# Two small SBUF tables get longer rows, so that every large tile behind them starts on a multiple of 128 bytes

## The chip, the cores and the metric

One Trainium2 chip, one of its cores. The metric is the time of one execution on the device in microseconds (us). Inputs are laid out in memory on the host before the launch; that is not timed.

## The reference

Three blocks in a row work on 256 tokens of 1024 features, all in float32. The first block has two layers. Layer 0 is differential attention over 256 context tokens and the 256 tokens themselves, layer 1 is a pooling over windows of tokens; each is followed by a SwiGLU network, and both are modulated by vectors made from a condition `c`. The second block mixes a gated linear attention and a block-sparse attention, and is followed by a wide network (1024 to 4096 and back) and a gated embedding.

```python
x = layer_norm(ALPHA * x + g1 * y_lat, ...)                # attention or pooling
x = layer_norm(ALPHA * x + g2 * swiglu(modulate(x, sh2, sc2), ffn_w_in[i], ffn_w_out[i]), ...)
...
x = x + (sigmoid(gate_a) * y_a + sigmoid(gate_b) * y_b) @ w_out
x = x + square(relu(rms_norm(x) @ w_up)) @ w_down
x = x + sigmoid(rms_norm(x) @ w_ple_gate) * (p @ w_ple)
```

## The kernel before

Nearly all the time goes into products of a 256-row activation with a large weight matrix. To get float32 accuracy from TensorE's faster float32 type (`f32r`, printed as f32 in the rows), every factor is split into a high and a low part, and a product is three matmuls: high by high, high by low, low by high.

- **Weights** stream from memory into a ring `raw` (six slots of 2048 floats per partition; the queue of SyncE, SP, issues these transfers in the order of use). ScalarE rounds a piece to its high part `wH` (line 638), VectorE subtracts and writes the low part `wL` (line 1213). A piece ("sub") is 128 x 1024.
- **Activations** are transposed by TensorE and split in the same way into a pair of tiles. `aHL` holds high and low part of the 1024-feature activations of most stages; `cH`, `cL` those of the context; `hH`, `hL` the hidden activations of SwiGLU (22 blocks of 128 features); `uH`, `uL` those of the wide network (32 blocks); `oa` and `pH`, `pL` two smaller ones.
- **Two ways to multiply.** In `three` (lines 2068 to 2070) the activation is the stationary operand (128 columns of it are loaded as weights, LDWEIGHTS, engine PEld in the rows) and 512 columns of the weight matrix stream past as the moving operand. In `columns_T` (lines 2103 to 2105, 256 columns) and `chunk_mm_halves` (lines 2136 and 2138) it is the other way round: a piece of `wH` or `wL` is stationary and the activations move.

```python
def three(outp, xh, xl, h, l, first, last_, part_of=False):
    T.matmul(outp, xh, h, ...)             # line 2068
    T.matmul(outp, xh, l, ...)             # line 2069
    return T.matmul(outp, xl, h, ...)      # line 2070
```

The first operand after the output is the stationary one. A row of the trace names them in another order: `ps<-wH,hH` at line 2068 is a matmul with `hH` stationary and `wH` moving; at line 2103, `ps<-cH,wH` has `wH` stationary and `cH` moving.

The stages in order: q, k, v of the attention (v with `cH` and `aHL` by turns, 192 matmuls), attention heads, its output product, `in0` and `out0` (SwiGLU of layer 0), pooling, `in1` and `out1`, the input product `win` of the second block with the linear attention in between, `bra` with the sparse attention in between (its stationary tile is `oa`), `brb`, `wo2`, `up`, `down` (stationary `uH`, `uL`), `pg`, `ple` (stationary `pH`, `pL`). `out0` and `out1` have `hH`, `hL` stationary. `rows_mm` runs those with an activation stationary: per block of 128 features and per half of the tokens two times three matmuls.

Between two matmuls that belong to a stage TensorE waits only for `w_lo` (VectorE has split the sub), for the transposed activations (`t_lo`, `h_lo`) and for a free bank of PSUM (`acc_out`). `idle_mm` (line 2222) issues matmuls of `hH` by `hH` whose result is not used, where TensorE would stand still at the end of a layer norm.

**Where tiles stand.** The tiles are allocated in the order of the code, each at the next multiple of 32 bytes behind the one before; some share their place with tiles of other stages. The built program has them at these bytes of a partition, modulo 128:

| tiles | before | after |
|---|---|---|
| `raw`, `wL`, `wH`, `aHL`, `x`, `cst` (in front of the two tables) | 0 | 0 |
| `modraw`, `lnp`, `tf`, `modrow`, `modcol` (behind `cols`) | 96 | 0 |
| `cb`, `cT`, `wPool1`, `v`, `qT`, `kT`, `cH`, `cL`, `ot`, `ex`, `mod0`, `sh1b`, `sc1b`, `wPool0`, `hH`, `hL`, `sh` (behind `cols` and `vcol`) | 32 | 0 |
| second block: `xn`, `oa`, `laH`, `laL`, `tabr`, `u`, `uH`, `uL`, `hu`, `pH`, `pL`, `gate` (behind `cols`) | 96 | 0 |

Of the kernel before, what the change touches and what calls it, by code (L numbers as in the profile page):

```python
# [34 lines left out]
P = 128  # L35
D = 1024
KT = D // P
# [56 lines left out]
VECS = [(0, 2), (0, 3), (0, 4), (0, 5), (1, 0), (1, 1), (1, 2), (1, 3), (1, 4), (1, 5)]  # L94
# [107 lines left out]
def build(nc, a, cst_d, pool_d, out):  # L202
    ctx = ExitStack()
    with ctx:
        def sem(name):
            return ctx.enter_context(nc.semaphore(name))

        def sb(stack, name, shape, dt=fp32):
            return stack.enter_context(nc.sbuf_tensor(name, shape, dt))
# [12 lines left out]
        eps = sb(ctx, "eps", [P, 2])  # L222
        bn = sb(ctx, "bn", [P, TT, 12])
        mv = sb(ctx, "mv", [P, TT, 2])
        cols = sb(ctx, "cols", [P, 113])

        gcol = sb(ctx, "gcol", [P, 82])

# [6 lines left out]
        sA = ExitStack()  # L235
# [11 lines left out]
        esum = modrow[:, 0:32].rearrange("p (m r) -> p m r", m=2)  # L247
        einv = modrow[:, 32:48]
        modcol = sb(sA, "modcol", [P, 2, 4, KT, 2])
        vcol = sb(sA, "vcol", [P, len(VECS) * KT])  # L250
        cb = sb(sA, "cb", [P, D])
        bcol = cols[:, 16:112]
        cT = sb(sA, "cT", [P, KT, 32])
# [118 lines left out]
        ctx_in, cols_in, cst_in, cst2_in = (sem(n) for n in ("ctx_in", "cols_in", "cst_in", "cst2_in"))  # L372
# [248 lines left out]
        def _(act):  # L621
# [68 lines left out]
                nc.scalar.activation(modrow[:, :], ps[:, 6, :], ACT.Copy).then_inc(mod_row, 1)  # L690


            act.dma_start(cols[:, :], a["cols"]).then_inc(cols_in, 16)
            act.dma_start(cst[:, 0:C_DIST], cst_d[:, 0:C_DIST]).then_inc(cst_in, 16)
            act.wait_ge(cols_in, 16)
            act.wait_ge(cT_zero, 1)
# [2063 lines left out]
```

## Time and profile before

| | before |
|---|---|
| median of three runs | 1114.23 us (1114.17 to 1116.12) |
| the profiled execution, its own time | 1114.73 us |
| its span, from the first to the last instruction | 1113.0 us |
| TensorE busy (share of the span) | 1099.3 us (99%) |
| VectorE, ScalarE busy | 776.3 us (70%), 587.0 us (53%) |
| granted TensorE clock | 0.999, that is its 2.4 GHz level all through |
| moved by DMA | 238.31 MB, 214 GB/s in the mean |

A busy row of PE reaches from a matmul's start to its modelled end, and matmuls overlap: what counts for the time is the distance from one start to the next, called pitch below. A matmul of 512 columns streams for 512 / 2.4 GHz = 213.3 ns, one of 256 for 106.7 ns.

### The profile page before, as it was taken

What the parts mean: (1) busy time and instruction counts of PE and PEld (TensorE: products, weight loads), DVE (VectorE), ACT (ScalarE), POOL (GpSimd) and SP (SyncE); (2) the same over time, 40 slices, a digit from 0 to 9 for tenths busy, and PEclk for the clock granted to TensorE, in tenths of its full rate; (3) what the DMA queues carried; (4) which work ended last, traced back from release to release, by engine and by line L of the source; (5) the groups of instructions that cost most, each with busy time, mean ns of one, the idle gap of its engine ahead of it and who ended that gap; (6) DMA issues with size and microseconds to landing.
All of it is one profiled execution on the core that took longest, in us unless ns stands there. A gap on an engine that the chain in (4) does not pass through costs nothing.

```text
span 1113.0 us, 14486 instructions
## 1 busy us (share of the span) xinstructions
PE 1099.3 (99%) x5851; PEld 910.0 (82%) x5851; DVE 776.3 (70%) x1007; ACT 587.0 (53%) x821; POOL 61.4 (6%) x118
## 2 busy tenths in 40 slices
PE   8999999999999999999999999999999999999998
PEld 4688766899998887888887878878888888888886
DVE  2596588889889797877745865455566677774454
ACT  3742376563454347555534767556754466563342
POOL 0011200002121001000000000000000000000000
PEclk9999999999999999999999999999999999999999
DMA  9987740679999946667567788786524455555541
GB/s 363 403 309 249 243 163 1 208 255 349 379 383 332 350 146 232 224 211 269 183 199 126 223 177 190 155 180 134 177 76 152 152 196 203 207 189 189 189 161 38
DMA packets 111986, 238.31 MB, mean 214 GB/s; under 512 B 5712, under 2 KB 51920, under 8 KB 110640
## 3 DMA queue, kind: packets, MB, share of 16 engines
q1 hardware_dynamic: 97280, 185.42, 53.2%
q0 software_dynamic: 14352, 51.72, 13.1%
q8 instruction: 46, 0.75, 0.3%
q10 hardware_dynamic: 288, 0.26, 0.1%
q14 instruction: 20, 0.16, 0.0%
HBM read 236.29 MB, written 1.07 MB: 213 GB/s over the span
## 4 chain that ended last, share of the span: by engine, by line
PE 92%; DVE 3%; DMA 3%; ACT 1%; issue 0%; SPq 0%; ACTq 0%
PE ps L2068 19%; PE ps L2069 19%; PE ps L2070 19%; PE ps L2136 10%; PE ps L2138 5%; PE ps L2105 4%; PE ps L2104 4%; PE ps L2103 4%; PE ps L2253 2%; DMA raw<-in_attn_w_qkv 2%; PE ps L2388 1%; PE ps L2356 1%; DMA raw<-in_qkv_first 1%; DVE wL L1213 1%; PE ps L2277 0%; PE ps L2621 0%
## 5 line engine op out<-in xcount | busy, mean ns | idle before, releaser
L1213 DVE TENSOR_TENSOR wL<-raw,wH 128x1024 fp32r<-128x1024 f32 x326 | 394.7, 1222 | 211.3 <-ACT wH L638 208.9
L638 ACT ACTIVATE wH<-raw 128x1024 fp32r<-128x1024 f32 x326 | 340.3, 1058 | 300.4 <-PE ps L2070 196.1
L2068 PE MATMUL ps<-wH,aHL 128*128 128x512 f32 x576 | 229.3, 398 | 2.4 <-DVE aHL L1616 0.9
L2069 PE MATMUL ps<-wL,aHL 128*128 128x512 f32 (+1 forms) x592 | 229.0, 387 | 0.0
L2070 PE MATMUL ps<-wH,aHL 128*128 128x512 f32 x576 | 224.8, 390 | 0.0
L2136 PE MATMUL ps<-aHL,wH 128*128 128x512 f32 x480 | 168.8, 397 | 0.0
L2068 PEld LDWEIGHTS ps<-wH,aHL 128*128 128x128 f32 x576 | 108.1, 188 | 35.1 <-issue 7.1
L2138 PE MATMUL ps<-aHL,wL 128*128 128x256 f32 x480 | 134.1, 279 | 0.0
L2069 PEld LDWEIGHTS ps<-wL,aHL 128*128 128x128 f32 x592 | 111.3, 188 | 20.8
L2070 PEld LDWEIGHTS ps<-wH,aHL 128*128 128x128 f32 x576 | 108.1, 188 | 23.4
L2136 PEld LDWEIGHTS ps<-aHL,wH 128*128 128x128 f32 x480 | 90.1, 188 | 21.7
L1289 DVE SCALAR_TENSOR_TENSOR modraw<-modraw,cb 128x1024 f32<-128x1024 f32 x80 | 96.4, 1219 | 4.4 <-DMA modraw<-in_mod_rows 4.3
L2138 PEld LDWEIGHTS ps<-aHL,wL 128*128 128x128 f32 x480 | 90.5, 188 | 0.0
L2103 PE MATMUL ps<-aHL,wH 128*128 128x256 f32 x288 | 81.7, 284 | 0.0
L2105 PE MATMUL ps<-aHL,wL 128*128 128x256 f32 x288 | 81.5, 283 | 0.0
L2104 PE MATMUL ps<-aHL,wH 128*128 128x256 f32 x288 | 81.5, 283 | 0.0
L2068 PE MATMUL ps<-wH,hH 128*128 128x512 f32 x176 | 70.0, 397 | 0.0
L2069 PE MATMUL ps<-wL,hH 128*128 128x512 f32 x176 | 69.6, 395 | 0.0
L2070 PE MATMUL ps<-wH,hL 128*128 128x512 f32 x176 | 69.2, 393 | 0.0
L555 POOL DMA_DIRECT2D modraw<-in_mod_rows x80 | 42.4, 531 | 367.8 <-DVE modraw L1289 313.4
L2103 PEld LDWEIGHTS ps<-aHL,wH 128*128 128x128 f32 x288 | 55.3, 192 | 0.0
L2104 PEld LDWEIGHTS ps<-aHL,wH 128*128 128x128 f32 x288 | 55.3, 192 | 0.0
(330 smaller groups left out, 1491.7 us busy)
## 6 DMA issues: line engine op xcount, KB each, us to landing
raw<-in_ffn_w_in SPq DMA_DIRECT2D x88, 512.0 KB
modraw<-in_mod_rows POOLq DMA_DIRECT2D x80, 512.0 KB, 6.6
raw<-in_w_in SPq DMA_DIRECT2D x32, 1024.0 KB
raw<-in_ffn_w_out SPq DMA_DIRECT2D x22, 1024.0 KB
raw<-in_w_up SPq DMA_DIRECT2D x16, 1024.0 KB
raw<-in_w_down SPq DMA_DIRECT2D x16, 1024.0 KB
mod<-in_mod_first SPq DMA_DIRECT2D x8, 1024.0 KB, 16.8
raw<-in_attn_w_qkv SPq DMA_DIRECT2D x8, 1024.0 KB
```

The source lines that it names most:

```text
L555: pool.dma_start(modraw[:, n % MT, :], a["mod_rows"][v, k, :, :]).then_inc(mod_in[n % MT], 16)
L638: nc.scalar.activation(wHigh(n), raw[:, (n // 2) % RAW, (n % 2) * 1024:(n % 2) * 1024 + 1024], ACT.Copy).then_inc(w_hi, 1)
L1213: V.tensor_tensor(wL[:, n % WL, :], raw[:, (n // 2) % RAW, (n % 2) * 1024:(n % 2) * 1024 + 1024], wHigh(n).bitcast(fp32), ALU.subtract).th ...
L1289: V.scalar_tensor_tensor(out=tile, in0=tile, scalar=1.0, in1=cb[:, :], op0=ALU.mult, op1=ALU.mult, accum_out=vcol[:, n:n + 1]).then_inc(ve ...
L2068: T.matmul(outp, xh, h, start=first, stop=False, skip_group_check=part_of)
L2069: T.matmul(outp, xh, l, start=False, stop=False, skip_group_check=part_of)
L2070: return T.matmul(outp, xl, h, start=False, stop=last_, skip_group_check=part_of)
L2103: T.matmul(dst, h, x_h[:, k, :], start=k == 0 and b % 2 == 0, stop=False, skip_group_check=True)
L2104: T.matmul(dst, h, x_l[:, k, :], start=False, stop=False, skip_group_check=True)
L2105: ins = T.matmul(dst, l, x_h[:, k, :], start=False, stop=k == KT - 1, skip_group_check=True)
L2136: T.matmul(dst, wH[:, slot(n + s), c0:c0 + P], aHL[:, k, :, :].rearrange("p a s -> p (a s)"), start=k == 0, stop=False, skip_group_check=True)
L2138: ins = T.matmul(dst[:, S:2 * S], wL[:, (n + s) % WL, c0:c0 + P], aH[:, k, :], start=False, stop=k == KT - 1, skip_group_check=True)
```

## The change

`cols` (a table of 113 floats per partition: condition and biases) gets rows of 128 floats, of which the transfer fills the first 113 as before; `vcol` (80 floats per partition) gets rows of 96. No instruction is added, removed or moved on any engine. What changes in the program is the row length of these two tables and the start of everything that is allocated behind them: by 32 bytes behind `cols`, by 96 bytes behind `cols` and `vcol`.

```diff
-        cols = sb(ctx, "cols", [P, 113])
+        cols = sb(ctx, "cols", [P, P])
...
-        vcol = sb(sA, "vcol", [P, len(VECS) * KT])
+        vcol = sb(sA, "vcol", [P, 96])
...
-            act.dma_start(cols[:, :], a["cols"]).then_inc(cols_in, 16)
+            act.dma_start(cols[:, 0:113], a["cols"]).then_inc(cols_in, 16)
```

## Rows read from the trace of the kernel before

**Rows 1.** Page: busy time by engine; chain that ended last, by engine
```profile
PE 1099.3 (99%) x5851; PEld 910.0 (82%) x5851; DVE 776.3 (70%) x1007; ACT 587.0 (53%) x821; POOL 61.4 (6%) x118
PE 92%; DVE 3%; DMA 3%; ACT 1%; issue 0%; SPq 0%; ACTq 0%
```

**Rows 2.** One tile's matmuls: count, duration in ns (min/median/max), first and last start
```profile
L2068 PE MATMUL ps<-wH,hH x176: 392/395/494, 340.6 to 609.3; 128*128 128x512 f32 x176
L2068 PE MATMUL ps<-wH,uH x128: 392/395/476, 989.7 to 1079.5; 128*128 128x512 f32 x128
L2068 PE MATMUL ps<-wH,cH x32: 394/394/500, 97.8 to 141.8; 128*128 128x512 f32 x32
```

**Rows 3.** Timeline of PE, 512 columns: start us, duration us, instruction
```profile
199.34 0.39 PE L2069 MATMUL ps<-wL,aHL 128*128 128x512 f32 x1
...
207.95 0.39 PE L2068 MATMUL ps<-wH,aHL 128*128 128x512 f32 x1
...
355.13 0.39 PE L2069 MATMUL ps<-wL,hH 128*128 128x512 f32 x1
...
366.33 0.39 PE L2069 MATMUL ps<-wL,hH 128*128 128x512 f32 x1
...
1020.03 0.40 PE L2069 MATMUL ps<-wL,uH 128*128 128x512 f32 x1
...
1031.46 0.39 PE L2070 MATMUL ps<-wH,uL 128*128 128x512 f32 x1
```

**Rows 4.** Timeline of PE in v, where cH and aHL alternate
```profile
103.34 0.39 PE L2068 MATMUL ps<-wH,cH 128*128 128x512 f32 x1
...
106.14 0.40 PE L2068 MATMUL ps<-wH,aHL 128*128 128x512 f32 x1
...
108.67 0.40 PE L2070 MATMUL ps<-wH,aHL 128*128 128x512 f32 x1
```

**Rows 5.** Timeline of PE, 256 columns, in k, in0 and the pooling
```profile
50.01 0.28 PE L2103 MATMUL ps<-cH,wH 128*128 128x256 f32 x1
...
52.39 0.28 PE L2105 MATMUL ps<-cH,wL 128*128 128x256 f32 x1
...
300.07 0.28 PE L2104 MATMUL ps<-aHL,wH 128*128 128x256 f32 x1
...
308.95 0.28 PE L2103 MATMUL ps<-aHL,wH 128*128 128x256 f32 x1
...
410.48 0.28 PE L2068 MATMUL ps<-wPool,aHL 128*128 128x256 f32 x1
...
412.83 0.28 PE L2070 MATMUL ps<-wPool,aHL 128*128 128x256 f32 x1
```

**Rows 6.** Timeline of PE, first matmuls of 512 columns after transposes or small ones
```profile
196.96 0.48 PE L2068 MATMUL ps<-wH,aHL 128*128 128x512 f32 x1
...
199.11 0.39 PE L2068 MATMUL ps<-wH,aHL 128*128 128x512 f32 x1
...
404.26 2.54 PE L2222 MATMUL ps<-hH 128*128 128x512 f32 x10
```

**Rows 7.** Windows: stretch and its length, busy us of the engines, clock, DMA share, GB/s
```profile
989.70:1079.90 90.20, 90.20 (x393) 72.61 (x392) 43.57 (x41) 38.18 (x45) 0.00 (x0) 1.00 0.54 189
```

**Rows 8.** Timeline of DVE with its wait in brackets; longest waits (us in total, times, longest)
```profile
402.69 0.69 DVE L1548 TENSOR_TENSOR sh<-ps,g2b 128x512 f32<-128x512 f32 x1 [1.24 <-PE ps L2070]
...
DVE sh L1493 <- PE ps L2070: 9.0, 1, 9.0
```

**Rows 9.** Page, costliest groups: VectorE on tiles at 0 and at 96
```profile
L1213 DVE TENSOR_TENSOR wL<-raw,wH 128x1024 fp32r<-128x1024 f32 x326 | 394.7, 1222 | 211.3 <-ACT wH L638 208.9
L1289 DVE SCALAR_TENSOR_TENSOR modraw<-modraw,cb 128x1024 f32<-128x1024 f32 x80 | 96.4, 1219 | 4.4 <-DMA modraw<-in_mod_rows 4.3
```

**Rows 10.** Windows early in the kernel (columns as in rows 7, DVE, ACT, POOL included)
```profile
20.00:25.00 5.00, 5.00 (x32) 3.12 (x24) 1.78 (x4) 3.07 (x6) 0.00 (x0) 1.00 1.03 423
60.00:65.00 5.00, 5.00 (x39) 4.72 (x38) 5.00 (x6) 2.01 (x2) 0.00 (x0) 1.00 1.04 398
```

## The prediction

> **What bounds the kernel now.** I read the page first: TensorE is busy 99% of the span and makes up 92% of the chain that ended last; VectorE has 3% of it, DMA 3% [rows 1]. A change that touches no instruction can therefore bring something only if it changes how fast one matmul follows another, or one of the few places where the chain leaves TensorE. Busy time does not tell that, since matmuls overlap. So I went to the timeline of PE, picked stretches without any other instruction between the matmuls, and divided the time between two starts by the number of steps. In the built program nothing differs but start addresses, so I sorted the stretches by where their operands start.
>
> For 512 moving columns the reader is to see two levels [rows 3]. Between 199.34 and 207.95 us lie 38 steps with `aHL` stationary and `wH`, `wL` moving, all at 0 modulo 128: 8.61 / 38 = 226.6 ns a step. Between 355.13 and 366.33 lie 48 steps with `hH`, `hL` stationary (32 modulo 128): 11.20 / 48 = 233.3 ns. Between 1020.03 and 1031.46 lie 49 steps with `uH`, `uL` stationary (96 modulo 128): 11.43 / 49 = 233.3 ns. The moving operand is the same ring in all three, and the function is the same. In v the two kinds stand side by side [rows 4]: from the first matmul with `cH` at 103.34 to the first with `aHL` at 106.14 it is 12 steps in 2.80 us, 233.3 ns; the next 11, with `aHL`, take 2.53 us, 230.0 ns, so they start slow and end fast. The difference is thus 6.7 ns a matmul, 2.9%, and it comes with a stationary tile that does not start on a multiple of 128 bytes. It hardly comes with the load on other engines: in `down` VectorE is busy only 43.57 of 90.20 us and DMA 54% [rows 7], less than over the whole kernel for VectorE [rows 1], and the step is still the slow one.
>
> What exactly the address does can't be read. Two readings fit: (a) a weight load of 512 bytes per partition that starts off a 128-byte line costs 6.7 ns more; (b) it costs that when stationary and moving operand stand differently modulo 128. A third, (c), is that the address modulo 128 has nothing to do with it, and the tiles that lie further back in SBUF are slower, since all the slow ones lie behind byte 116,000 and `aHL` and the weights in front. There is one weak witness. `idle_mm` has both operands in `hH`, far back and both at 32. Ten of them after small matmuls take 2.54 us, less the 0.39 us of the last one's own duration 2.15 us for nine steps; nine steps with everything at 0 after transposes take 199.11 - 196.96 = 2.15 us too [rows 6]. Nine steps at the slow level would be 9 x 6.7 = 0.06 us more than at the fast one (less while such a run settles), so this speaks for (b) and against (c), by a difference of a few hundredths. (a) and (b) give the same after the change, since everything then stands at 0.
>
> **The change part by part.** Sum against the profiled execution, 1114.73 us, 0.5 us over the median of the three runs. The stationary tiles that move from 32 or 96 to 0:
>
> - `out1`: half of the `hH` matmuls. Rows 2 has 176 at line 2068; lines 2069 and 2070 have as many, 528 in all, 264 in each layer. 264 x 6.7 ns = 1.77 us. VectorE's first step behind it waits 9.0 us for TensorE [rows 8], so all of it counts.
> - `out0`: the same 1.77 us, but at its end VectorE's step on the last accumulators waits only 1.24 us for TensorE [rows 8]; if TensorE comes 1.77 us earlier, VectorE is late next, with the half before. I take 1.24 us.
> - `down`: 3 x 128 = 384 matmuls [rows 2], 2.57 us. TensorE is busy 90.20 of 90.20 us there [rows 7], and it is on the chain.
> - v: 3 x 32 = 96 matmuls with `cH` [rows 2], 0.64 us; and the 96 with `aHL` that alternate with them go from 230.0 to 226.6 ns [rows 4], 0.33 us.
> - `bra`, with `oa` stationary: 8 blocks x 2 halves x 2 x 3 = 96 matmuls by the code. The attention steps in between break them into runs of about twelve, and after a break even aligned ones step 2.15 / 9 = 239 ns at first [rows 6]. I take half, 0.3 us.
> - `ple`: 24 matmuls by the code, 0.16 us.
>
> Against it: where an activation moves, unlike starts seem no harm. 256 columns with `cH` moving (32) over `wH` (0) step 2.38 / 20 = 119.0 ns, with `aHL` (0) over `wH` (0) 8.88 / 74 = 120.0 ns; in the pooling, with `wPool` at 32 moving in two of three, 2.35 / 20 = 117.5 ns [rows 5]. If all become 120.0: 192 x 1.0 + 48 x 2.5 ns = 0.3 us lost. `in0`, `in1`, `up`, `win`, `brb`, `wo2` and `pg` have both operands in front of the tables and stay as they are.
>
> VectorE, ScalarE: an operation on tiles at 96 takes 1219 ns, one on tiles at 0 takes 1222 [rows 9], and these engines are 4% of the chain; nothing, covered by TensorE, and if it were not, 3 ns of 1222. DMA: while the transfers into `mod0` (32) and `lnp` (96) run among those into `raw`, 423 GB/s are moved, and 398 with `raw` alone as the target [rows 10]; the starts do not hurt, so nothing is to be had. The two tables themselves are read at the same width as before.
>
> Sum: 1.77 + 1.24 + 2.57 + 0.64 + 0.33 + 0.3 + 0.16 - 0.3 = 6.7 us. 1114.73 - 6.7 = 1108.0 for an execution like the profiled one, and **1107.5 us** from the median. Bounds of this case: all of `out0` and `bra` (0.9 us more) and no loss for moving operands (0.3 more) gives 1106.3; if `bra`, `ple` and the `aHL` part of v give nothing and `out0` half, 5.3 us, it is 1108.9.
>
> **The rivals.**
> - *The saving is partly taken back* by a wait. For: in `out0` the margin is the 1.24 us named, and weights arrive just in time in places. Against: in `down`, 2.57 us are in the clear. If `out0` and v gave nothing, 2.2 us of the 6.7 would be lost; with one more such place, `out1`, 4.0: from 1109.7 to 1111.5, say 1109 to 1112.
> - *No change.* Reading (c), or another property of the slow tiles. For: no row shows a tile that lies far back and starts at 0 modulo 128. Against: rows 6, weakly, and that tiles at 125,000 (`uH`) and at 204,000 bytes (`cH`) step alike. Time: 1114.2, or 1114.5 with the small loss above. The Trainium skill (SBUF — State Buffer, Door 1: The DMA port swizzle) has a rule that would also end here: SBUF is read in lines of 16 bytes, and what costs is to cross into a new line. By that rule a weight row of 512 bytes touches 32 lines from 0, 32 or 96 alike, no alignment beyond 16 bytes is worth anything, and the time stays 1114.2; the two levels in rows 3 are nothing that it explains.
> - *Slower.* Equal starts are what costs, and the 6.7 ns are of the place. For: the three 256-column rows, where the unlike ones are up to 2.5 ns faster than the like ones [rows 5]. For 512 columns that is up to 5 ns, on the 1128 matmuls with a moved stationary tile 5.6 us, and 0.3 us as above: 1120.1. It decides from 2.2 / 1128 = 2.0 ns a matmul. Against: rows 3 have the like pair faster by 6.7 ns at the very shape in question.
>
> **How the numbers follow.** A measurement of this kernel tells about 0.2% (2.2 us) from no change. The forecast 0.67 (its own range 1106 to 1109); partly taken back 0.14; no change 0.13; slower 0.04; and 0.02 for more gain than I see. Faster than 1112.0: 0.67 + 0.14 + 0.02 = 0.83; the same 0.13; slower 0.04. The range for 8 in 10 takes the forecast with its bounds and most of the second case: 1105.5 to 1111.5.
>
> **What the profile after would show.** 233.3 ns becomes 226.7 in `out0`, `out1` and `down`, the median duration of line 2068 with `hH` falls from 395 towards that of `aHL`, the matmuls with `aHL` stay as they are, and with `cH` moving the step becomes 120.0. `down` would last 90.2 - 2.6 = 87.6 us. The prediction is wrong if `uH` and `hH` keep their 233.3 ns (then it is the place), or if they reach 226.7 and TensorE shows new waits after `out0` or before the attention.

## The result and the profile after

| | before | after |
|---|---|---|
| median, same chip | 1114.9 us (1114.17 to 1116.12, 4 runs) | 1107.8 us (1106.66 to 1109.29, 4 runs) |
| the profiled execution, its own time and span | 1114.73, 1113.0 us | 1107.73, 1106.0 us |

The ratio is 0.9936, with an interval of 0.9919 to 0.9953: 7.1 us or 0.6% faster. A second measurement beside the experiments below gave 1106.63 us against 1114.97, 0.993 (0.9916 to 0.9943).

The page of after, busy time by engine and the chain that ended last, by engine, beside [rows 1]:

```profile
PE 1092.8 (99%) x5851; PEld 910.7 (82%) x5851; DVE 776.0 (70%) x1007; ACT 586.7 (53%) x821; POOL 61.6 (6%) x118
PE 87%; DVE 6%; DMA 4%; ACT 1%; SPq 1%; issue 1%; ACTq 0%; DVEq 0%
```

TensorE lost 6.5 us of its busy time; VectorE, ScalarE and the counts stand as before. The same matmuls of after as in [rows 2], count and duration in ns:

```profile
L2068 PE MATMUL ps<-wH,hH x176: 389/389/501, 339.4 to 605.1; 128*128 128x512 f32 x176
L2068 PE MATMUL ps<-wH,uH x128: 389/389/476, 985.3 to 1072.6; 128*128 128x512 f32 x128
L2068 PE MATMUL ps<-wH,cH x32: 389/389/499, 97.5 to 140.6; 128*128 128x512 f32 x32
```

The median fell from 394 or 395 to 389 ns. The steps say it better. PE's timeline of after: 48 steps in `out0`, 48 in `down`, 12 with `cH` and 12 with `aHL` in v, then 20 steps of 256 columns with `cH` moving and 20 in the pooling (for [rows 3 to 5]):

```profile
349.67 0.39 PE L2069 MATMUL ps<-wL,hH 128*128 128x512 f32 x1
...
360.55 0.39 PE L2069 MATMUL ps<-wL,hH 128*128 128x512 f32 x1
...
1009.82 0.39 PE L2068 MATMUL ps<-wH,uH 128*128 128x512 f32 x1
...
1020.70 0.39 PE L2068 MATMUL ps<-wH,uH 128*128 128x512 f32 x1
...
102.93 0.39 PE L2068 MATMUL ps<-wH,cH 128*128 128x512 f32 x1
...
105.65 0.39 PE L2068 MATMUL ps<-wH,aHL 128*128 128x512 f32 x1
...
108.37 0.39 PE L2068 MATMUL ps<-wH,cH 128*128 128x512 f32 x1
...
50.00 0.28 PE L2104 MATMUL ps<-cL,wH 128*128 128x256 f32 x1
...
52.40 0.28 PE L2103 MATMUL ps<-cH,wH 128*128 128x256 f32 x1
...
407.51 0.28 PE L2069 MATMUL ps<-wL,aHL 128*128 128x256 f32 x1
...
409.90 0.28 PE L2068 MATMUL ps<-wPool,aHL 128*128 128x256 f32 x1
```

The reader is to see 10.88 / 48 = 226.7 ns in `out0` and in `down` (before 233.3), 2.72 / 12 = 226.7 in v both with `cH` and with `aHL`, 2.40 / 20 = 120.0 with `cH` moving and 2.39 / 20 = 119.5 in the pooling. The window over `down` of after, beside [rows 7]:

```profile
985.30:1073.00 87.70, 87.70 (x393) 72.74 (x392) 43.58 (x41) 38.01 (x45) 0.00 (x0) 1.00 0.55 194
```

The same 393 matmuls with the engine never idle, 2.5 us sooner. From the first start of a stage's matmuls to the last, by the two traces, v went from 44.52 to 43.61 us (0.91), `out0` from 61.64 to 60.11 (1.53), `out1` from 62.25 to 60.53 (1.72), `bra` from 35.02 to 34.77 (0.25), `down` from 90.23 to 87.73 (2.50), `ple` from 5.37 to 5.21 (0.16). That is 7.07 us. The first weight product began 0.40 us earlier, at 16.05 us (the traces of this study have it between 16.05 and 16.70). By the starts of corresponding matmuls 0.4 us went back in the layer norm behind `out1`. There TensorE loads blocks of `x` to transpose them; before, that load came without a wait, after, it waits for VectorE (line 1512). The rows of PEld, before and after:

```profile
618.52 1.02 PEld L2253 LDWEIGHTS ps<-cst,x 128*128 128x128 f32 x8
```

```profile
614.72 0.86 PEld L2253 LDWEIGHTS ps<-cst,x 128*128 128x128 f32 x8 [0.40 <-DVE x L1512]
```

Another 0.2 us went back at the start of `in1` and 0.2 us came in at the start of `up`, where the matmuls of lines 2136 and 2138 changed their pace (more on them at the end). What is left over is 0.1 us. The span is 7.0 us shorter.

VectorE at the end of `out0`, beside [rows 8], wait in brackets:

```profile
396.82 0.68 DVE L1548 TENSOR_TENSOR sh<-ps,g2b 128x512 f32<-128x512 f32 x1
...
398.26 0.69 DVE L1556 BATCH_NORM_STATS2 bn<-x 128x6 f32<-128x512 f32 x1
...
399.96 0.69 DVE L1548 TENSOR_TENSOR sh<-ps,g2b 128x512 f32<-128x512 f32 x1 [1.00 <-PE ps L2070]
```

The last accumulators are taken 2.73 us earlier than before (402.69 then), and VectorE still waited 1.00 us for them. The 1.24 us of before were no limit: the work of VectorE ahead of that wait had come forward as well (the same step of line 1548 one half earlier started at 399.32 before and starts at 396.82 here). At its start, on the other hand, `out0` lost a little, since TensorE now waits there for VectorE to multiply the last hidden block (line 1737). PE of after:

```profile
341.14 0.50 PE L2068 MATMUL ps<-wH,hH 128*128 128x512 f32 x1 [0.17 <-DVE sh L1737]
```

### The profile page after: what moved, and what is told of

Read it like the earlier page. It is cut to its first block, busy times and chain, and to the rows that moved or that the text cites. A ratio compares the mean times of both kernels' runs of the same rounds, so it can differ in the third digit from the quotient of the medians.

```text
span 1106.0 us, 14486 instructions
## 1 busy us (share of the span) xinstructions
PE 1092.8 (99%) x5851; PEld 910.7 (82%) x5851; DVE 776.0 (70%) x1007; ACT 586.7 (53%) x821; POOL 61.6 (6%) x118
## 4 chain that ended last, share of the span: by engine, by line
PE 87%; DVE 6%; DMA 4%; ACT 1%; SPq 1%; issue 1%; ACTq 0%; DVEq 0%
PE ps L2068 19%; PE ps L2070 18%; PE ps L2069 18%; PE ps L2136 10%; PE ps L2138 5%; PE ps L2105 2%; PE ps L2104 2%; PE ps L2103 2%; DVE wL L1213 2%; PE ps L2253 2%; DMA raw<-in_qkv_first 2%; PE ps L2388 1%; PE ps L2356 1%; DMA raw<-in_ffn_w_in 1%; DMA raw<-in_w_in 1%; DVE modraw L1289 1%
## 5 line engine op out<-in xcount | busy, mean ns | idle before, releaser
L1213 DVE TENSOR_TENSOR wL<-raw,wH 128x1024 fp32r<-128x1024 f32 x326 | 395.1, 1222 | 207.1 <-ACT wH L638 204.5
L1289 DVE SCALAR_TENSOR_TENSOR modraw<-modraw,cb 128x1024 f32<-128x1024 f32 x80 | 96.5, 1219 | 3.9 <-DMA modraw<-in_mod_rows 3.8
```

The source lines that it names most:

```text
L1213: V.tensor_tensor(wL[:, n % WL, :], raw[:, (n // 2) % RAW, (n % 2) * 1024:(n % 2) * 1024 + 1024], wHigh(n).bitcast(fp32), ALU.subtract).th ...
L1289: V.scalar_tensor_tensor(out=tile, in0=tile, scalar=1.0, in1=cb[:, :], op0=ALU.mult, op1=ALU.mult, accum_out=vcol[:, n:n + 1]).then_inc(ve ...
```

## The experiments

d is from here on the start of an activation tile less the start of the ring (`wH` and `wL` are alike), modulo 256 bytes. In the kernel before d is 0 for `aHL`, -96 for `hH` and `cH`, -32 for `uH`, `oa`, `pH`; in after it is 0 for all. The kernels add unused tiles, or use a tile from a few floats further back; none leaves work out. Each added line shifts the line numbers by one. First four kernels on the question of the two readings (a) and (b).

**Everything moved by 32 bytes**, after with one pad in front of all:

```diff
+        sb(ctx, "pad0", [P, 8])
         sLow = ExitStack()
```

> The changed kernel with a pad of 32 bytes in front of everything: all large tiles, the weight ring and aHL included, stand at 32 modulo 128, so every stationary tile is off the 128-byte line but equal to its moving operand. Theory (a), a weight load that starts off a 128-byte line costs 6.7 ns: the 1728 matmuls of 512 columns with aHL stationary and the 1128 with the other activations step 233.3 instead of 226.7 ns, 19 us more, and those with the ring stationary lose as well: 1127 us or more. Theory (b), what costs is a stationary and a moving operand at unequal places modulo 128: all steps stay 226.7 and 120.0 ns, 1107.8 us. Theory (c), the place in SBUF: already contradicted by the change itself, would give 1107.8 too.

Measured: 1108.58 us (1106.52 to 1109.68), ratio to before 0.994 (0.9925 to 0.9954). All settled 512-column steps were 226.7 ns though no large tile stood on a multiple of 128 bytes. Reading (a) fell.

**The first edit alone**, made in the kernel before; `vcol` keeps its 80 floats:

```diff
-        cols = sb(ctx, "cols", [P, 113])
+        cols = sb(ctx, "cols", [P, P])
...
+            act.dma_start(cols[:, 0:113], a["cols"]).then_inc(cols_in, 16)
```

> Only cols is padded: the tiles of the second block (oa, uH, uL, pH, pL) stand at 0, those behind vcol (cH, cL, hH, hL, wPool0) at 64 modulo 128. If the unit is 128 bytes, down, bra and ple are fast (2.57 + 0.3 + 0.16 = 3.0 us less than before) and out0, out1 and v keep a step of about 233.3 ns: about 1111.8 us. If 64 bytes are enough, hH and cH step 226.7 too: 1107.8 us.

Measured: 1109.66 us (1108.11 to 1112.9), ratio 0.9956 (0.9941 to 0.9972). `uH` (d = 0) stepped 226.7 ns, `hH` and `cH` (d = -64) 228.9. With `cH` moving six of eight stretches stepped 117.8 and two 113.4, 116.7 in the mean. So there are more than two levels.

**The ring alone at 32**, after with 8 floats in front of `raw` and 24 behind `wH`:

```diff
+        sb(ctx, "pad0", [P, 8])
         sLow = ExitStack()
...
+        sb(ctx, "pad1", [P, 24])
```

> The changed kernel with the ring raw, wL, wH at 32 and everything else, aHL, hH and uH included, at 0 modulo 128. In lines 2068 to 2070 the stationary operand is then on the line and the moving one is not. Theory (a): they all step 226.7 ns; the ring is stationary in 1056 matmuls of 256 columns and 960 of lines 2136 and 2138, where up to 6.7 ns each are lost, 13.5 us: 1107.8 to 1121 us. Theory (b): 1728 + 1128 matmuls step 233.3 ns, 19 us more, and the 256-column ones of lines 2103 to 2105 step about 119 instead of 120.0 ns, 1 us less: 1126 us.

Measured: 1124.85 us (1124.43 to 1125.56), ratio 1.0088 (1.0073 to 1.0103). The activations stood on multiples of 128 bytes as in after; the two pads had pushed them by 128 bytes, so d is 96 for all of them. The timeline of PE in this kernel, 38 steps with `aHL` and 48 with `uH` stationary:

```profile
198.15 0.40 PE L2071 MATMUL ps<-wL,aHL 128*128 128x512 f32 x1
...
207.06 0.39 PE L2070 MATMUL ps<-wH,aHL 128*128 128x512 f32 x1
...
1017.43 0.39 PE L2070 MATMUL ps<-wH,uH 128*128 128x512 f32 x1
...
1028.68 0.39 PE L2070 MATMUL ps<-wH,uH 128*128 128x512 f32 x1
```

8.91 / 38 = 234.5 and 11.25 / 48 = 234.4 ns, where only the moving operand had moved. Reading (b) holds in kind.

**`aHL` alone at 32**, after with 8 floats in front of `aHL` and 24 behind it:

```diff
+        sb(ctx, "pad0", [P, 8])
         aHL = sb(ctx, "aHL", [P, KT, 2, S], f32r)
+        sb(ctx, "pad1", [P, 24])
```

> The changed kernel with aHL alone at 32, everything else at 0 modulo 128. Both theories (a) and (b): the 1728 matmuls with aHL stationary, 226.7 ns in both kernels so far, step 233.3 ns, 11.5 us more: 1119 us, which gives the cost a second time and in front part of SBUF. Where aHL moves (lines 2103 to 2105) (b) expects 119 instead of 120.0 ns, 1 us less, (a) no difference. Theory (c), the place: 1107.8.

Measured: 1117.94 us (1117.44 to 1119.8), ratio 1.0028 (1.0016 to 1.004). The timeline of PE, 38 steps with `aHL`, 48 with `hH` stationary:

```profile
198.24 0.40 PE L2072 MATMUL ps<-wH,aHL 128*128 128x512 f32 x1
...
207.11 0.40 PE L2071 MATMUL ps<-wL,aHL 128*128 128x512 f32 x1
...
352.61 0.40 PE L2072 MATMUL ps<-wH,hL 128*128 128x512 f32 x1
...
363.76 0.40 PE L2072 MATMUL ps<-wH,hL 128*128 128x512 f32 x1
```

`aHL` at 233.4 ns was expected; `hH` at 11.15 / 48 = 232.3 was not. The pads had pushed it and `uH` by 128 bytes, so they stood where (b) asks, alike modulo 128, and were slow. The unit is wider than I had written. The next kernels look for the period, with pads that put each group of tiles at a d of its own.

**d = 64, 256, 128** for `aHL`, first block, second block in after:

```diff
+        sb(ctx, "pad0", [P, 16])
         aHL = sb(ctx, "aHL", [P, KT, 2, S], f32r)
+        sb(ctx, "pad1", [P, 48])
...
+        sb(sB, "pad2", [P, 96])
```

> The changed kernel with pads only, so that the large tiles stand at chosen distances from the ring wH, wL (d = start of the tile less start of the ring, modulo 512): aHL at d = 64, cH, hH and wPool0 at d = 256, oa, uH, pH and laH at d = 128. Theory: the step of 512 columns follows d modulo 256. Then hH and cH stationary step 226.7 ns as at d = 0, uH again 232.4 as the tiles at d = 128 did in the run with aHL at 32, and aHL something near the 228.9 that d = -64 gave. Time about 1107.8 + 1728 x 2.2 ns + 504 x 5.7 ns - 864 x 3.3 ns (256 columns moving, if d = 64 gives 116.7 as d = -64 did) = 1111.6 us. Rival one: d counts modulo 512 or as the distance itself; then hH and cH are unlike too and step 232 to 234 ns, 3.6 us more, about 1115. Rival two: only multiples of 128 count and the 232.4 had another cause (the place): hH and uH both 226.7, about 1108.7.

**d = 256, 96, 64** for the same three groups:

```diff
+        sb(ctx, "pad0", [P, 64])
         aHL = sb(ctx, "aHL", [P, KT, 2, S], f32r)
+        sb(ctx, "pad1", [P, 64])
...
+        sb(sA, "pad2", [P, 24])
...
+        sb(sB, "pad3", [P, 16])
```

> The changed kernel with pads only: aHL at d = 256 from the ring, cH, hH, wPool0 at d = 96, oa, uH, pH at d = 64. Theory (d modulo 256): aHL stationary 226.7 and moving 120.0 as before; hH, cH 234.3 as the run with the ring at 32 gave for d = 96, 624 x 7.6 ns = 4.7 us; uH, oa, pH the same as aHL gives at d = 64 in the kernel beside it, near 228.9, 504 x 2.2 ns = 1.1 us: about 1113.6 us. Rival (modulo 512 or the distance itself): aHL is unlike at 232 to 234 ns, 1728 x 5.7 ns = 9.9 us more, about 1123.

Measured: 1118.44 us (1117.84 to 1120.17), ratio 1.0031 (1.0019 to 1.0043), and 1114.83 us (1114.29 to 1115.45), 0.9997 (0.9988 to 1.0006). The timeline of PE in the first of them, `hH` at d = 256, and of the second, `aHL` at d = 256 and `uH` at 64:

```profile
352.54 0.39 PE L2073 MATMUL ps<-wH,hL 128*128 128x512 f32 x1
...
363.42 0.39 PE L2073 MATMUL ps<-wH,hL 128*128 128x512 f32 x1
```

```profile
199.65 0.39 PE L2073 MATMUL ps<-wL,aHL 128*128 128x512 f32 x1
...
208.27 0.39 PE L2072 MATMUL ps<-wH,aHL 128*128 128x512 f32 x1
...
1012.60 0.40 PE L2073 MATMUL ps<-wL,uH 128*128 128x512 f32 x1
...
1023.80 0.40 PE L2073 MATMUL ps<-wL,uH 128*128 128x512 f32 x1
```

10.88 / 48 = 226.7 and 8.62 / 38 = 226.8 ns: 256 bytes apart is as good as 0, for tiles in front and at the back, while 128 apart is not. So the period is taken to be 256, and "modulo 512" fell; of the other values of d none was tried again 256 bytes further. My guess that +64 would equal -64 fell too: 11.20 / 48 = 233.3 instead of 228.9. On the 1728 matmuls with `aHL` stationary that is 4.4 ns each or 7.6 us, about the 6.8 us by which the first of the two missed what I had expected.

**The second edit alone**, made in the kernel before:

```diff
-        vcol = sb(sA, "vcol", [P, len(VECS) * KT])
+        vcol = sb(sA, "vcol", [P, 96])
```

> The kernel before with the second edit alone: vcol gets rows of 96 floats, cols keeps its 113. All tiles behind cols then stand 32 bytes below the ring modulo 256 (d = -32), those of the second block as before. Theory (the difference of the starts sets the step): hH, cH and uH stationary all at 233.3 ns as at d = -32 and -96 before, so this edit alone brings nothing: 1114 to 1115 us, with the 256 columns of cH moving the only ones that may change (192 matmuls, 0.6 us at most). Rival (the two edits each bring a part, as rows of tiles nearer to a boundary): hH and cH get quicker, 1111 us or less.

Measured: 1113.93 us (1112.29 to 1115.82), ratio 0.9993 (0.9983 to 1.0003); `hH` and `uH` 233.3 as before, `cH` moving 118.1. Alone it brings nothing that can be told, the first brings 0.44%, both together 0.64%: the second edit only pays once the first has been made, since it closes the last 64 bytes. That rests on the steps: 624 matmuls with `hH`, `hL`, `cH`, `cL` stationary go from 228.9 to 226.7 ns, 1.4 us. By the times alone the intervals of the first edit and of both overlap.

**`aHL` at d = -64**, a candidate for something better than after, with the unchanged after once more as its measure:

```diff
+        sb(ctx, "pad0", [P, 112])
         aHL = sb(ctx, "aHL", [P, KT, 2, S], f32r)
+        sb(ctx, "pad1", [P, 16])
```

> The changed kernel with pads so that aHL alone stands 64 bytes below the ring modulo 512, all else as far from the ring as in the changed kernel. A candidate for a better placement: where aHL is stationary (1728 matmuls) 228.9 instead of 226.7 ns is expected, 3.8 us lost; where it moves, 864 matmuls of 256 columns at 116.7 instead of 120.0, 2.9 us gained, and the pairs at lines 2136 and 2138 in in1 at 173.3 instead of 176.7 ns a matmul, up to 1.6 us gained. Theory (the difference of the two starts sets the step): 1107 to 1109 us, no difference that can be told from the changed kernel. Rival (the values of d = -64 seen so far belong to those tiles, not to the difference): aHL steps 233 ns stationary, as at +32, and the time is 1112 or more.

> The changed kernel once more, on the same chip and in the same rounds as the three with pads, as the value that they are to be held against. Every theory expects 1107 to 1109 us and a ratio to the kernel before of 0.992 to 0.995.

Measured: 1112.78 us (1111.98 to 1114.34) against 1106.63 (1106.34 to 1109.61) for after, 6 us slower. The steps were as good as hoped or better: 228.9 ns with `aHL` stationary, and 8.39 / 74 = 113.4 ns where it moves in `in0` (after: 120.0; the first 96 matmuls of `in0` stepped 117.8). TensorE reached the end of `in0` 5 us earlier than in after, and lost it there. PE's timeline of the candidate:

```profile
335.98 0.39 PE L2072 MATMUL ps<-wH,hL 128*128 128x512 f32 x1
341.87 0.79 PE L2070 MATMUL ps<-wH,hH 128*128 128x512 f32 x1 [5.51 <-DVE sh L1739]
342.46 0.63 PE L2071 MATMUL ps<-wL,hH 128*128 128x512 f32 x1
342.89 0.63 PE L2072 MATMUL ps<-wH,hL 128*128 128x512 f32 x1
```

Its DVE timeline just before, and its windows over the wait and the matmuls behind it (the column 1.00, 0.50 is the granted clock):

```profile
340.01 1.21 DVE L1215 TENSOR_TENSOR wL<-raw,wH 128x1024 fp32r<-128x1024 f32 x1
341.14 0.67 DVE L1739 TENSOR_TENSOR sh<-sh,ps 128x512 f32<-128x512 f32 x1
```

```profile
342.00:347.50 5.50, 5.50 (x13) 4.33 (x14) 4.82 (x7) 1.54 (x2) 0.53 (x1) 0.50 0.64 233
348.50:354.00 5.50, 5.50 (x26) 4.54 (x25) 4.92 (x7) 2.12 (x2) 0.54 (x2) 1.00 0.69 246
```

The same step of VectorE in after, run again on this chip:

```profile
341.21 0.68 DVE L1737 TENSOR_TENSOR sh<-sh,ps 128x512 f32<-128x512 f32 x1
```

And PE's first matmul behind it there, which waited 0.54 us and kept its clock:

```profile
341.95 0.50 PE L2068 MATMUL ps<-wH,hH 128*128 128x512 f32 x1 [0.54 <-DVE sh L1737]
```

VectorE multiplied the last hidden block at 341.14 us in the one and at 341.21 in the other, and it has no gap before it: it, not TensorE, ends `in0`. Matmuls 6 ns shorter only bring TensorE there earlier. In the candidate TensorE stood still for 5.51 us, and then the granted clock was 0.50, the 1.2 GHz level: the starts from 342.46 on are 0.43 us apart instead of 0.23. Fourteen such steps cost 14 x 0.2 = 2.8 us more than the wait. By the starts of corresponding matmuls the candidate was 4.8 us ahead at 335 us and 2.8 behind at 354. The rest, about 5 us to the end, comes from the stages with `aHL` stationary, and from the pairs at lines 2136 and 2138, which ran at 176.7 ns a matmul where after, run again, had 173.3. My hope for these pairs did not come true in this trace; since after itself has them at 176.7 in one trace and at 173.3 in the other, one trace per placement can't say what the distance does to them. No placement was found that beats after.

**Starts off the 32-byte grid**, `hH`, `hL` from 16 bytes, `uH`, `uL` from 4 bytes on:

```diff
-        hH = sb(sF, "hH", [P, F1 // P, S], f32r)
+        hH = sb(sF, "hH", [P, F1 // P * S + 64], f32r)[:, 4:4 + F1 // P * S].rearrange("p (k s) -> p k s", s=S)
```

> The changed kernel, with hH and hL used from 16 bytes behind a multiple of 256 and uH and uL from 4 bytes behind one (d = 16 and d = 4); nothing else moves. So far every start was a multiple of 32 bytes. Theory one, the two operands are compared in units of 32 bytes or more: 226.7 ns for both, about 1107.5 us, unless a row that begins inside a unit and so touches one more costs something of its own. Theory two, any difference counts: about 233 ns for both, (528 + 384) x 6.6 ns = 6.0 us more, about 1113.5 us. Rival, the Trainium skill (SBUF — State Buffer, Door 1: The DMA port swizzle), lines of 16 bytes of which only the number touched counts: nothing for hH, and something for uH, whose rows of 512 bytes then touch 33 lines instead of 32: hH 226.7, uH above it.

Measured: 1112.16 us (1109.53 to 1114.28), ratio 0.9975 (0.9965 to 0.9986). The timeline of PE, 48 steps in `out0` and 48 in `out1`, both with `hH` at d = 16:

```profile
354.34 0.39 PE L2070 MATMUL ps<-wH,hL 128*128 128x512 f32 x1
...
365.22 0.39 PE L2070 MATMUL ps<-wH,hL 128*128 128x512 f32 x1
...
562.63 0.40 PE L2070 MATMUL ps<-wH,hL 128*128 128x512 f32 x1
...
573.83 0.40 PE L2070 MATMUL ps<-wH,hL 128*128 128x512 f32 x1
```

10.88 / 48 = 226.7 in the one stage and 11.20 / 48 = 233.3 in the other, at the same addresses, each through the whole stage. `uH` at d = 4 stepped 232.3. So a difference of 4 bytes already costs, and at 16 bytes the same instructions have two steady paces. The Trainium skill's lines of 16 bytes (SBUF — State Buffer, Door 1: The DMA port swizzle) fit `uH`, whose rows touch one line more, and `hH` in `out0`. They don't explain the 233.3 ns in `out1`: rows that begin 16 bytes further touch as many lines as before.

**Only the low parts at 32**, after with `hL` and `uL` used from 8 floats on:

```diff
-        hL = sb(sF, "hL", [P, F1 // P, S], f32r)
+        hL = sb(sF, "hL", [P, F1 // P * S + 64], f32r)[:, 8:8 + F1 // P * S].rearrange("p (k s) -> p k s", s=S)
```

> The changed kernel, with only the low parts hL and uL used from 32 bytes further back (d = 32), the high parts hH and uH at d = 0. The three matmuls of a product have hH, hH, hL stationary. Theory: the cost belongs to a load of an unlike stationary tile and the columns that stream past while it is loaded; then one matmul in three pays, 226.7 + 6.6 / 3 = 228.9 ns in the mean for both families, with the longer step beside line 2070, and the time is 1107.5 + 912 x 2.2 ns = 1109.5 us. Rival (unlike operands anywhere in the sequence put the whole pipeline out of step): 233 ns for all three, 6 us more, 1113.5 us.

Measured: 1113.26 us (1112.08 to 1114.54), ratio 0.9985 (0.9975 to 0.9994). The timeline of PE, one product and the next:

```profile
1030.11 0.40 PE L2069 MATMUL ps<-wL,uH 128*128 128x512 f32 x1
1030.35 0.39 PE L2070 MATMUL ps<-wH,uL 128*128 128x512 f32 x1
1030.57 0.40 PE L2068 MATMUL ps<-wH,uH 128*128 128x512 f32 x1
1030.81 0.40 PE L2069 MATMUL ps<-wL,uH 128*128 128x512 f32 x1
```

A product lasts 0.70 us, as with all three stationary tiles unlike, and not the 0.687 that one payer in three would make. In the mean over `down` the step beginning at line 2069, ahead of the matmul that has `uL`, is the long one (239 ns), but the other two (228 and 233) do not fall back to 226.7. Which of the three is long says little by itself, since in the kernel before, with all three tiles unlike, it is the same one (237, against 231 and 232, in `out1`). The theory that each load pays for itself fell: one unlike tile in three makes the whole product as slow as three.

## Why the prediction was right, point by point

- **1107.5 us forecast, 1107.8 measured; 6.7 us forecast, 7.1 measured** (7.0 in the span). The step from 233.3 to 226.7 came as said in every stage named, `aHL` stayed at 226.7, and the operations of [rows 9] take 1222 and 1219 ns after as before, though `modraw` moved.
- `out1` 1.77 forecast, 1.72 measured; `down` 2.57 and 2.50 (its window 87.7 us for a forecast 87.6); v 0.97 and 0.91; `bra` 0.3 and 0.25; `ple` 0.16 and 0.16; the steps with an activation moving went to 120.0 ns as said, but of the 0.3 us priced for them the starts show 0.05 us in the pooling and nothing that can be told in k.
- **The mis-sized term is `out0`**: I cut 1.77 to 1.24 us because VectorE waits only 1.24 us for TensorE at its end. 1.53 us were kept, and the wait went from 1.24 to 1.00 only. A wait at one place is a margin only if what the waiting engine did before is tied to nothing that moves. Here it is tied: on the page of after most of VectorE's idle time ahead of a split ends with ScalarE's rounding, and most of ScalarE's ahead of a rounding with a matmul of TensorE, so both came forward.

```profile
L1213 DVE TENSOR_TENSOR wL<-raw,wH 128x1024 fp32r<-128x1024 f32 x326 | 395.1, 1222 | 207.1 <-ACT wH L638 204.5
L638 ACT ACTIVATE wH<-raw 128x1024 fp32r<-128x1024 f32 x326 | 340.0, 1057 | 297.3 <-PE ps L2070 186.6
```

- **"Partly taken back"** did not occur at its size (1109 to 1112), but in kind, and at places that I had not named: 0.17 us by the wait for VectorE at the start of `out0`, most of what `out0` fell short of its 1.77, and 0.4 us behind `out1`, of which I had said that all of it counts because VectorE waits 9.0 us for TensorE at its end. That wait was no proof for the next step: VectorE came 3.80 us earlier to the transposes of `x`, TensorE 4.20 us. Without the start 0.40 us earlier, which no term had and which is luck, the span would have become 6.6 us shorter, still close to the 6.7 of the forecast.
- **Which reading**: (c) fell, since the same far tiles reach 226.7. (a) fell with everything at 32. (b) was right that the two operands must start alike, and wrong about modulo 128: the period is 256. The forecast didn't notice, because the two pads take `hH` from -96 and `uH` from -32 to 0 modulo 256 as well. Had they brought them to 128, it would have been 232.3 ns, and nearly no gain by a change that does all it says. That risk stood in none of my rivals; the 0.13 for no change was for other reasons.
- **"Slower, equal starts cost"** fell for 512 columns. For 256 columns it is partly true: 113 to 119 ns in most unlike places (120.0 at d = 96) against 120.0.
- **The Trainium skill's rule of 16-byte lines** (SBUF — State Buffer, Door 1: The DMA port swizzle), as I had applied it in the rival for no change, would have left 1114.2; the measured 1107.8 contradicts that.

What is not settled is the mechanism. The steps by distance, in the table below, are all that the runs show. The Trainium skill (SBUF — State Buffer, A bandwidth-pool intuition that's wrong (but worth ruling out)) gives the loading of weights a read port of its own, independent of the moving operand's. If that were all, one would not expect that moving the ring alone brings the steps from 226.7 to 234.4 ns, and that moving everything brings nothing. So the pace depends on the two operands together. Whether their reads meet in SBUF or somewhere else, no run here shows.

## What to carry to other kernels

When a kernel is bound by TensorE, measure its steps from start to start by tile, and sort them by the distance between where the stationary and the moving operand begin; make that distance a multiple of 256 bytes, not merely each start a multiple of 128. This was measured for `f32r` with 128 x 128 stationary and 512 moving columns, each matmul with its own load; other types and shapes were not tried, and for 256 columns the order is another. A pad can be worth nothing while another is still missing, as that of `vcol` was, so set the distances together and read the addresses from the built program. And before making a stage's matmuls still shorter, look for who ends the stage: in `in0` it was VectorE, and arriving 5 us early cost 2.8 us more than it gave, through the clock.

## What the runs showed that was not expected

Step in ns by d (activation less ring, bytes modulo 256), settled stretches; 512 columns with the activation stationary, 256 columns with it moving:

| d | 512, stationary | 256, moving |
|---|---|---|
| 0 (also at 256) | 226.7 | 120.0 |
| 4 | 232.3 | |
| 16 | 226.7 in one stage, 233.3 in another | |
| 32 | 233.3 | 117.8, then 116.7 |
| 64 | 233.3 | 117.8 |
| 96 | 234.3 | 120.0 |
| 128 | 232.3 | 118.6 |
| 160 (-96) | 233.3 | 119.0 |
| 192 (-64) | 228.9 | 117.8 or 113.4, both with `cH` and with `aHL` |
| 224 (-32) | 233.3 | 118.1 |

- The best place for a stationary tile is, with d = 96, the worst for a moving one of 256 columns, though by 1 to 6 ns only. At d = -64 a moving tile has two paces: `cH` stepped 117.8 in six stretches and 113.4 in two, `aHL` 117.8 in its first 96 matmuls and 113.4 in all later ones.
- Two steady paces at the same addresses occur with a stationary activation as well, `hH` at d = 16 (226.7 and 233.3), and in the pairs of lines 2136 and 2138 at d = 0: 176.7 ns a matmul through `in1` in after and 173.3 when it was run again, but 173.3 through `up` in both. So one execution can have both. What chooses between them was not tried; by the starts of corresponding matmuls it makes 1.7 us over `in1` (454 to 558 us) in the candidate against after run again, within the spread of the runs of one kernel.
- The clock granted to TensorE fell to 0.50 behind a stop of 5.51 us in the candidate with `aHL` at -64, and came back after some fourteen matmuls; in after, run again, with a stop of 0.54 us at the same place, the steps behind it are 0.23 us.
